# Up projection of a first feed-forward: one 512-column product for both operand halves

## What is computed

```
h2 = modulate(rmsnorm(x, norm2_g), shift, scale)
z = (h @ w_up).reshape(b, rows, cols, 2 * D_FF)          # 1024 -> 5632
z = lax.conv_general_dilated(z, conv_w, (1, 1), 'SAME', feature_group_count=2 * D_FF)   # 3 x 3, per channel
z = z.reshape(b, l, 2 * D_FF) + conv_b
return (silu(z[..., :D_FF]) * z[..., D_FF:]) @ w_down    # 2816 -> 1024
```

## Time and profile before

| | us |
|---|---|
| median of 3 runs (lowest to highest) | 864.97 (864.18 to 865.75) |
| profiled execution: span of its instructions (the page gives no other time of it) | 863.4 |
| PE busy | 844.9 (98%) |
| DVE busy | 592.5 (69%) |
| ACT busy | 477.8 (55%) |
| POOL busy | 437.0 (51%) |

### The profile page before, as it was taken

How to read it: one execution, slowest core, us unless ns; L and a number is a source line. 1 busy time by engine, 2 the same in 40 slices (tenths; PEclk the granted TensorE clock), 3 DMA queues, 4 the chain that set the end, 5 groups by cost and what they waited for, 6 DMA issues and landing times.

```text
span 863.4 us, 15200 instructions
## 1 busy us (share of the span) xinstructions
PE 844.9 (98%) x6034; PEld 781.1 (90%) x6034; DVE 592.5 (69%) x1196; ACT 477.8 (55%) x794; POOL 437.0 (51%) x210
## 2 busy tenths in 40 slices
PE   7999999999999999999999999999999999999996
PEld 1488899999799999999999988999999899999996
DVE  4897979867667896767677879586447554444455
ACT  4542345442656665555555864555437766666665
POOL 4775512223662488888887300200000788888881
PEclk9999999999999999999999999999999999999998
DMA  9967565655376456666565556254536466656551
GB/s 343 357 243 241 181 227 195 232 172 186 124 241 217 154 172 193 194 174 193 174 192 173 160 153 195 93 194 126 168 98 197 146 196 176 198 180 195 180 171 50
DMA packets 45755, 160.89 MB, mean 186 GB/s; under 512 B 5218, under 2 KB 5490, under 8 KB 45556
## 3 DMA queue, kind: packets, MB, share of 16 engines
q1 hardware_dynamic: 45680, 159.91, 57.7%
q10 hardware_dynamic: 4, 0.01, 0.0%
HBM read 158.85 MB, written 1.05 MB: 185 GB/s over the span
## 4 chain that ended last, share of the span: by engine, by line
PE 87%; DVE 5%; DMA 3%; ACT 3%; issue 1%; POOL 0%; SPq 0%; DVEq 0%; ACTq 0%
PE bank L652 14%; PE bank L657 14%; PE bank L655 13%; PE bank L1031 9%; PE bank L1037 5%; PE bank L1072 4%; PE bank L1070 4%; PE bank L1068 4%; DVE wlo L512 2%; PE bank L930 2%; DMA ada_sc<-in_ada 2%; PE bank L754 1%; PE bank L756 1%; PE bank L760 1%; DMA ada_buf<-in_adaT 1%
## 5 line engine op out<-in xcount | busy, mean ns | idle before, releaser
L512 POOL TENSOR_TENSOR wlo<-raw,whi 128x1024 fp32r<-128x1024 f32 (+1 forms) x171 | 399.3, 2353 | 376.0 <-ACT whi L1280 375.8
L1280 ACT ACTIVATE whi<-raw 128x1024 fp32r<-128x1024 f32 (+1 forms) x253 | 258.1, 1026 | 60.6 <-PE bank L657 23.2
L1707 DVE SCALAR_TENSOR_TENSOR accs<-bank,vec,accs 128x189 f32<-128x189 f32 (+4 forms) x440 | 161.2, 433 | 71.2 <-ACT accs L1571 71.2
L652 PE MATMUL bank<-h,whi 128*128 128x256 f32 x504 | 143.7, 286 | 0.0
L657 PE MATMUL bank<-h,whi 128*128 128x256 f32 x504 | 142.3, 283 | 0.0
L655 PE MATMUL bank<-h,wlo 128*128 128x256 f32 x496 | 140.5, 283 | 0.6 <-DVE wlo L512 0.6
L512 DVE TENSOR_TENSOR wlo<-raw,whi 128x1024 fp32r<-128x1024 f32 x82 | 99.1, 1220 | 17.5 <-ACT whi L1280 16.8
L652 PEld LDWEIGHTS bank<-h,whi 128*128 128x128 f32 x504 | 96.6, 192 | 0.7 <-issue 0.3
L657 PEld LDWEIGHTS bank<-h,whi 128*128 128x128 f32 x504 | 96.7, 192 | 0.0
L655 PEld LDWEIGHTS bank<-h,wlo 128*128 128x128 f32 x496 | 95.1, 192 | 1.0 <-DVE wlo L512 0.9
L1068 PE MATMUL bank<-gh,whi 128*128 128x256 f32 x320 | 90.6, 283 | 0.0
(11 more groups left out here) (350 smaller groups left out, 1808.2 us busy)
## 6 DMA issues: line engine op xcount, KB each, us to landing
raw<-in_up SPq DMA_DIRECT2D x88, 512.0 KB, 3.6
raw<-in_w_in SPq DMA_DIRECT2D x45, 512.0 KB, 4.1
raw<-in_down SPq DMA_DIRECT2D x44, 512.0 KB, 3.6
ada_kT<-in_adaT SPq DMA_DIRECT2D x22, 512.0 KB, 3.9
raw<-in_w_out SPq DMA_DIRECT2D x16, 512.0 KB, 4.4
raw<-in_w_in_t SPq DMA_DIRECT2D x12, 512.0 KB, 4.4
ada_vM<-in_adaT SPq DMA_DIRECT2D x10, 512.0 KB, 4.1
ada_buf<-in_adaT SPq DMA_DIRECT2D x8, 512.0 KB, 12.3
```

What stands on the lines that cost most here:

```text
L512: return e.tensor_tensor(wlo[:, j % HL, 0:k], raw[:, j % RAW, 0:k], whi[:, j % HL, 0:k].bitcast(F32), ALU.subtract)
L652: e.matmul(ps, wh[:, k, :], xh(k), start=k == 0, stop=False)
L1280: e.activation(whi[:, j % HL, 0:(k1 - k0) * 128], raw[:, j % RAW, 0:(k1 - k0) * 128], ACT.Copy).then_inc(S.hi.up(j))
L1707: return e.scalar_tensor_tensor(out=out, in0=a, scalar=s, in1=b, op0=o1, op1=o2)
```

## The change

The first feed-forward takes the form of the second. `up_pair` is gone; `wide_pair` and `lin_wide` serve both. The chunks, their order and the slabs stay as they are. Pair 0 is no longer cut in parts. Banks are handed out by `pair_banks`: three for gates, one for values from pair 3 on. After the stage, `lin_ring` goes on from where it stood before it, with the events at which the stage's last users free the four banks. ACT gets `low_part` for both chunks of a pair and splits the chunk that used to follow `silu` already ahead of the centre taps; DVE gets two additions per pair.

```diff
-                lin(up, i, banks[slot][:, 0:L], x, free, late=i == 1)
-                lin(up, i + NFF, banks[slot][:, L:2 * L], x)
...
+            def lin_wide(f, n, ps, free, beside=None):
...
+                    else:
+                        w.wait_ge(S.h2h, k)
+                        w.wait_ge(S.h2l, k)
                     e.matmul(ps, wh[:, k, :], M["h2"][:, k, :, :].rearrange("p v t -> p (v t)"), start=k == 0,
...
+            def pair_banks():
+
+                order = [(lin_ring.n + i) % 4 for i in range(4)]
+                ring = Ring(3)
+                ring.until = [lin_ring.until[s] for s in order[:3]]
+                return order, ring, lin_ring.until[order[3]]
+
+            def wide_pair(f, i, order, ring, last_free):
+                slot, free = ring.take(i, S.gl, (f, i))
+                gate_bank[f, i] = order[slot]
+                lin_wide(f, i, banks[gate_bank[f, i]], free)
...
                 if i < 3:
+                    slot, free = aux_ring.take(("value", f, i), S.value, (f, i))
+                    value_bank[f, i] = banks[4 + slot]
                 else:
+                    value_bank[f, i], free = banks[order[3]], (S.value, (f, i - 1))
                     w.wait_ge(*last_free)
+                lin_wide(f, i + NFF, value_bank[f, i], free,
...
-            x = of("h2h", "h2l", S.h2h, lambda k: k, S.h2l, lambda k: k)
+            order, ring, last_free = pair_banks()
             for i in range(NFF):
-                up_pair(0, "up", i, x)
+                wide_pair(0, i, order, ring, last_free)
                 if i >= DLAG:
                     slab(0, "down", i - DLAG)
+            for s in order[:3]:
+                lin_ring.until[s] = ring.until[order.index(s)]
+            lin_ring.until[order[3]] = (S.value, (0, NFF - 1))
             slab(0, "down", NFF - 3)
             mem_key(4)
...
             def ffn(f, up, down):
                 w.wait_ge(S.conv, 0)
                 for i in range(NFF):
                     splits(ch(up, i) + HL)
-                    if f and i:
-                        low_part(i, 0)
+                    if i:
+                        low_part(f, i, 0)
                     splits(ch(up, i + NFF) + HL)
...
+                    if i == 0:
+                        low_part(f, i, 0)
+                    low_part(f, i, 1)
+                    splits(ch(up, i + NFF) + HL + 1)
+                    w.wait_ge(*((S.z2, (1, i)) if f else (S.value, (0, i))))
...
+                    both, value = up_bank(f, i)[:, :], value_bank[f, i]
+                    w.wait_ge(S.half, (f, i, 0))
+                    tt(both[:, 0:L], both[:, 0:L], M["sq"][:, i % 2, 0:L], ALU.add)
+                    w.wait_ge(S.half, (f, i, 1))
+                    t = tt(both[:, L:2 * L], value[:, 0:L], M["sq"][:, i % 2, L:2 * L], ALU.add)
+                    t.then_inc(S.value.up((f, i)))
+                    w.wait_ge(S.value, (f, i))
```

More of the change, by code:

```diff
@@ L411, in program @@
             kT = signal("kT", range(8))
-            half = signal("half", [(i, v) for i in range(NFF) for v in range(2)])
+            half = signal("half", [(f, i, v) for f in range(2) for i in range(NFF) for v in range(2)])
             h2h = signal("h2h", range(8))
@@ L473, in program @@
             ol = signal("ol", range(4))
-            value = signal("value", range(NFF))
-            z2 = signal("z2", range(NFF))
+            value = signal("value", FPAIRS)
+            z2 = signal("z2", [(1, i) for i in range(NFF)])
             y = signal("y", range(4))
@@ L1011, in pe @@
                 mem_key(j)
[L1013 to L1018, removed]
-                lin(up, i, banks[slot][:, 0:L], x, free, late=i == 1)
-                lin(up, i + NFF, banks[slot][:, L:2 * L], x)
-            def lin_wide(name, n, ps, free, beside=None):
+            def lin_wide(f, n, ps, free, beside=None):
+                name = "up2" if f else "up"
                 c = ch(name, n)
@@ L1244, in pe @@
             residual("wo", of("oh", "ol", S.oh, lambda k: k // 2, S.ol, lambda k: k // 2), 2, 6, lambda: mix(3))
[L1246 to L1249, removed]
+            order, ring, last_free = pair_banks()
             for i in range(NFF):
-                second_pair(i, gate_ring, banks[order[3]])
+                wide_pair(1, i, order, ring, last_free)
                 for n in behind(1, i):
@@ L1538, in cut, with low_part @@
                 e.activation(M["gh"][:, i % GRING, :], g_at(f, i), ACT.Copy).then_inc(S.gh.up((f, i)))
-            def low_part(i, v):
-                w.wait_ge(S.chunk, ch("up2", i + v * NFF))
+            def low_part(f, i, v):
+                w.wait_ge(S.chunk, ch("up2" if f else "up", i + v * NFF))
                 if i > 1:
-                    w.wait_ge(S.value, i - 2)
-                e.activation(M["sq"][:, i % 2, v * L:v * L + L], (value_bank[i] if v else up_bank(1, i))[:, L:2 * L],
-                             ACT.Copy).then_inc(S.half.up((i, v)))
+                    w.wait_ge(S.value, (f, i - 2))
+                e.activation(M["sq"][:, i % 2, v * L:v * L + L], (value_bank[f, i] if v else up_bank(f, i))[:, L:2 * L],
+                             ACT.Copy).then_inc(S.half.up((f, i, v)))
             def ffn(f, up, down):
@@ L2020, in ffn @@
                     tiles = [(i, 2 * i), (i + NFF, 2 * i + 1)]
-                    if f:
[L2022 to L2027, removed]
+                    both, value = up_bank(f, i)[:, :], value_bank[f, i]
[5 more added lines that the diff above has]
+                    w.wait_ge(S.value, (f, i))
+                    if f:
                         z = both.rearrange("p (v t) -> p v t", v=2)
-                        tt(z, z, M["rsd2"][:, :].unsqueeze(1).broadcast_to((128, 2, L)), ALU.mult).then_inc(S.z2.up(i))
+                        tt(z, z, M["rsd2"][:, :].unsqueeze(1).broadcast_to((128, 2, L)),
+                           ALU.mult).then_inc(S.z2.up((f, i)))
                     last = {}
```

27 lines of the change are left out of this document (6 added, 21 removed).

## The result

| us | before | after |
|---|---|---|
| median (lowest to highest) | 865.14 (864.18 to 865.75), 4 runs | **874.64** (872.75 to 876.35), 4 runs |
| ratio after to before, 95% interval | | 1.0114 (1.0102 to 1.0126) |
| span of the profiled execution | 863.4 | 873.3 |
| PE, DVE, ACT, POOL busy | 844.9, 592.5, 477.8, 437.0 | 845.8, 608.4, 487.3, 436.3 |

The account below looks back on a forecast made before the run. PE was taken to bound the first feed-forward. Terms -3.06 + 5.09 + 4.39 + 2.3 = +8.72 us on a span of 863.4 gave 872.1; with 1.5 for the median over the span, 873.7 us, range 870.7 to 876.2.

Parts of the forecast that it names:

- What bounds the kernel: First feed-forward: PE runs without a gap, 8.64 us per pair with slab before; DVE, ACT and POOL have room.
- Wide chunks: On PE, two wide-form chunks take 5.59 us instead of 5.76; 18 pairs after the first four gain 3.06 us.
- First pair: Pair 0 on PE: gate chunk waits for the last low half of h2, ending at 293.90 us, +0.78.
- Head wait: Before gate chunk 3, PE waits for `gl` of pair 0: a stall of 4.82 us, loss +5.09 at pair 3.
- Later pairs: After pair 3, DVE's loop of 7.94 us fits under PE's 8.47, so no second stall in the head.
- Tail wait: Before `mem_key(4)`, PE waits for `gl` of pair 21, whose bank it takes: a stall of 4.39 us.
- The clock: Granted clock falls in both stalls, each costing between nothing and 2.3 us; the middle, 1.15 each, taken: +2.3.
- It moves as a block: Everything behind `slabs` hangs on PE's own products and shifts by the same +6.42 us.
- the clock did not hold in either stretch: Rival: both stalls come, but the clock holds in both (871.4 us) or falls in one (872.6); chance 0.35 together.
- no engine but PE was the bound: Rival: DVE or ACT bounds the whole stage, with a loop above 8.47 us; some 883 us; chance 0.06.
- gate chunk 3 and `mem_key(4)` did not find their banks free: Rival: both chunks find their bank free, so neither stall comes; 862.2 us; chance 0.03.
- the wide form does save: Rival: wide form saves nothing on PE, so 18 x 0.17 us come back; 876.8 us; chance 0.04.

Follow-up runs that it names:

- Experiment 8: Changed kernel with pairs 0, 1, 2 and 21 in the old form, pair 0 in the other ring, `mem_key(4)` on gate 19's bank: 862.00 us, ratio 0.9964.
- Experiment 1: Changed kernel with `lin_ring` moved on one slot, so that `mem_key(4)` takes the bank of gate 19: 870.99 us, ratio 1.0065.
- experiment 5: Changed kernel with unused products added on PE, 11 before gate chunk 3 and 9 before `mem_key(4)`: 871.26 us, ratio 1.0066.
- experiments 7: Changed kernel with pairs 0 to 2 in the old form, gate 0 in the other ring, `mem_key(4)` on gate 19's bank: 863.97 us, ratio 0.9986.
- experiment 2: Changed kernel with gate 0 in the other ring, so that gate chunk 3 has a free bank; tail left as it was: 874.31 us, ratio 1.0106.
- experiment 6: Kernel before with `lin_ring` moved on by three, so that `mem_key(4)` takes the bank of pair 21: 867.78 us, ratio 1.0031.
- experiment 9: Kernel before, with POOL making the low half of one weight chunk (`w_in2`, 16) for only 128 of 1024 columns: 863.64 us, ratio 0.9977.
- experiment 4: Changed kernel with unused products added on PE, 18 before gate chunk 3 and 16 before `mem_key(4)`: 875.39 us, ratio 1.0126.

## Why the prediction was right, point by point

- **What bounds the kernel**: right. PE is full from pair 4 to slab 19, and a pair with slab takes 152.40 / 18 = 8.47, as forecast.
- **Wide chunks**: right; -3.12 for 18 pairs against -3.06. Experiment 8 leaves this term alone: 3.13 us less at `slabs` in its trace, 3.2 by the medians.
- **First pair**: +0.94 against +0.78. The last wide product was issued at 290.00 and not 289.93, and a low product followed it by 0.31, not 0.23.
- **Head wait**: the chain of hand-overs holds at each step. Forecast and measured: DVE's taps of pair 0 296.38 and 296.61, of pair 1 303.66 and 303.95, gate chunk 3 309.90 and 310.18; the stall by starts 4.82 and 4.95. 0.16 of the shift of 0.28 is pair 0's.
- **Later pairs**: covered, as forecast. DVE's round from pair 1's taps to pair 2's is 311.96 - 303.95 = 8.01 (forecast 7.94), and no second wait comes in the head.
- **Tail wait**: 4.39 forecast, 4.45 by starts. Experiment 1 shows that it is the bank's.
- **The clock**: it falls in both stretches, as forecast, but the term of 1.15 us each was **half of what came**: 2.36 and 2.32 in the profiled execution, the upper bound that was named (2.3). Experiment 1 has 1.67 for the one of the head, and experiment 5 gives 1.7 apiece by the medians, with about 1 us either way. The bound would have been the better value: behind the waits a wide product takes 3.58 / 8 = 0.45 us in place of 0.23 and one of 256 columns 0.21 in place of 0.12, until the clock is back.
- **"It moves as a block"**: this step failed. Behind `slabs` stood a DVE instruction that was held by POOL for 1.5 us, and two waits of PE that hung on it. They are off the path when the stage ends at another time against POOL's queue. The kernel before has this loss, the changed one has not; experiments 1, 7 and 8, in which the stage ends early again, have it once more (2.38 to 2.40 us for two `h`).
- The two errors, +2.4 and -1.5, partly cancel, so part of the closeness is luck: the prediction of 873.7 stands 0.9 under the 874.64 measured. The sum by its own terms was 8.72; the trace has 9.9. (What it added to the span, 1.5, is 864.97 - 863.4 = 1.57; with that the sum gives the 873.7.)
- **Rivals**: the clock did not hold in either stretch; no engine but PE was the bound; gate chunk 3 and `mem_key(4)` did not find their banks free; the wide form does save.
- What the prediction had not said is that the **list of banks and the late chain are two things**. It worked out the late chain and put the wait at the ring's fourth gate chunk; experiment 2 shows that a fourth bank only moves it by one pair, and experiments 7 and 8, which have that bank too, that it goes when the first pairs have the old form. In the tail it is the other way round: the bank of gate 19 alone takes away the wait (experiment 1), and the old form alone does not (experiment 6).

The Trainium skill (SBUF — State Buffer, Who interferes with whom) says that a DVE instruction with two inputs in SBUF contends with a GpSimd instruction that reads SBUF, and calls the pair of ports that they share an exclusive lock, where the order of issue decides which of the two is blocked. By that rule the 1.5 us could have been looked for ahead: the trace agrees, `h<-xc,fgm,h` (all operands in SBUF) takes 1.97 us under POOL's `wlo<-raw,whi` and 0.48 without it (experiment 9). The rows also agree with its counterpart for one input: `xc<-bank,mod,xc` and the taps, which read a PSUM bank beside SBUF, keep their length under POOL (two `xc` took 0.88 us at 487.65, when POOL had begun at 487.55).

## What to carry to other kernels

In this case a form of work that is cheaper on the bounding engine, but adds a hand-over to the one behind it, pays in the middle of a loop and costs at its ends, where the pipeline fills and drains. Here the first three rounds and the last got the old form, with one more bank at the start and, for the work behind the loop, a bank that is free earlier: 862.0 us in place of 874.6. The bank at the start alone only moves the place at which the leader meets a late follower. Price an idle stretch of TensorE of over 4 us in the midst of its work with its length and some 2 us of slow products behind it (1.5 to 2.4 in the traces here), and look behind the stage for instructions of DVE that run beside POOL, before assuming that all moves as a block.

## What was not expected of the hardware

- A float32 product of 256 columns from a 128 x 128 weight is two instructions, 0.21 us apart at a granted clock of 1.00 (36 for 18 products), where a product in the rounded format is one of 0.12.
- The price of a fall of the clock is not fixed: 2.36 and 2.32 us in one execution, 1.67 in another after an idle stretch of the same 4.79 us. After 4.33 us (experiment 2) the next chunk took 323.69 - 319.24 = 4.45, 1.66 too much. All six unfilled stretches of 4.28 to 4.79 us in the traces had a fall behind them (1.54 to 2.38 us), but the length of one stretch doesn't decide alone: after 3.00 us idle no fall was seen in one execution, and behind waits of only 0.44 and 0.71 us, with few products between them, there was one in experiment 8 and none before.
- The untouched work ahead of the stage ends anywhere from 287.53 to 291.59 us in the executions shown (in the last, of experiment 4, the clock was low from 229 to 233 us), while the stage behind repeats to a few hundredths (4.79 us of idle time in two kernels). Terms of a tenth can be read only from such a common point.
- One DVE instruction of 0.47 us grew to 1.97 beside POOL, and took 1.5 us of PE's time with it, though DVE is busy for only 69% of the span.
